# A transformer block kernel whose experts' second matrix becomes the moving operand, with tokens on the partitions

## The reference

```python
def _peer(h, w_q, sub_keys_1, sub_keys_2, expert_u, expert_v):
    ...                                   # choose 128 experts and gates per token
        u = expert_u[ix]
        v = expert_v[ix]
        a = jax.nn.gelu(jnp.einsum('td,thkd->thk', hx, u), approximate=False) * gx
        return jnp.einsum('thk,thkd->td', a, v)

    x = x + gate2 * _peer(h2, ...)        # end of the second block
return _rmsnorm(x, final_norm_g)          # mean of squares over 1024 features, then a gain

# linear attention: v is one quarter of the projection for each of 4 heads
proj = h @ w_in                           # gq, gk, gv, gr, glow, ..., iw, ...
```

## Time and profile before

| | us |
|---|---|
| median of three executions | 2174.11 |
| the profiled execution | 2175.14 |
| its span, first to last instruction | 2173.4 |
| TensorE busy | 2137.9 (98% of the span) |
| VectorE busy | 1609.3 (74%) |
| ScalarE busy | 967.6 (45%) |
| GpSimd busy | 401.8 (18%) |

### The profile page before, as it was taken

How to read it: one execution, slowest core, us unless ns; L and a number is a source line. 1 busy time by engine, 2 the same in 40 slices (tenths; PEclk the granted TensorE clock), 3 DMA queues, 4 the chain that set the end, 5 groups by cost and what they waited for, 6 DMA issues and landing times.

```text
span 2173.4 us, 30748 instructions
## 1 busy us (share of the span) xinstructions
PE 2137.9 (98%) x11787; PEld 1958.5 (90%) x11787; DVE 1609.3 (74%) x2958; ACT 967.6 (45%) x1689; POOL 401.8 (18%) x296
## 2 busy tenths in 40 slices
PE   8999989999999999999999999999999999999999
PEld 6877778887777788789999999999999999999998
DVE  4777556664976544799998897777667888888884
ACT  5444445444234423433364756766433333333333
POOL 2000110000000001000133333222223334443330
PEclk9999989999999999999999999999999999999999
DMA  7411135431231122124778888898999899999981
GB/s 257 148 50 40 49 128 192 170 136 61 104 106 41 51 85 97 64 95 146 256 279 282 307 290 284 302 314 292 333 355 385 345 375 365 370 374 376 375 334 57
DMA packets 137153, 471.07 MB, mean 217 GB/s; under 512 B 10080, under 2 KB 59488, under 8 KB 111280
## 3 DMA queue, kind: packets, MB, share of 16 engines
q1 hardware_dynamic: 45760, 283.96, 35.0%
q0 software_dynamic: 36864, 134.23, 16.4%
q10 hardware_dynamic: 54384, 50.92, 7.0%
HBM read 416.52 MB, written 52.43 MB: 216 GB/s over the span
## 4 chain that ended last, share of the span: by engine, by line
PE 84%; DVE 11%; ACTq 2%; ACT 1%; issue 1%; DMA 0%; SPq 0%; DVEq 0%
PE bank L156 83%; DVE whl L309 2%; ACTq L2235 2%; DVE L L1479 1%; DVE L L1477 1%; DVE row L2176 1%; DVE room L2120 1%; DVE room L2116 1%; PE bank L668 1%; DVE fg L2127 0%; PE bank L1568 0%; DMA XT<-in_xT 0%; DVE L L1460 0%; ACT whl L302 0%; DVE wk L1852 0%
## 5 line engine op out<-in xcount | busy, mean ns | idle before, releaser
L156 PE MATMUL bank<-xhl,whl 128*128 128x384 f32 (+1 forms) x5304 | 1092.3, 363 | 14.6 <-DVE whl L519 7.7
L156 PEld LDWEIGHTS bank<-xhl,whl 128*128 128x128 f32 x5304 | 948.9, 189 | 107.7 <-issue 11.0
L309 DVE TENSOR_TENSOR whl<-raw,whl 128x1024 fp32r<-128x1024 f32 (+2 forms) x389 | 469.1, 1215 | 254.1 <-ACT whl L302 208.5
L156 PE MATMUL bank<-ag,whl 128*128 128x384 f32 x3072 | 544.2, 340 | 1.3 <-ACT h_both L2231 1.3
L156 PEld LDWEIGHTS bank<-ag,whl 128*128 128x128 f32 x3072 | 542.1, 188 | 1.6 <-ACT h_both L2231 1.6
L302 ACT ACTIVATE whl<-raw 128x1024 fp32r<-128x1024 f32 (+2 forms) x389 | 398.0, 1034 | 217.7 <-PE bank L156 150.1
L2163 POOL DMA_INDIRECT row<-in_U_rows,row_at x128 | 182.1, 1423 | 607.6 <-DVE row L2176 432.3
L2163 POOL DMA_INDIRECT row<-in_V_rows,row_at x128 | 178.5, 1395 | 268.3 <-DVE y_tok L2192 236.3
L2192 DVE SCALAR_TENSOR_TENSOR y_tok<-row,row_a,y_tok 128x1024 f32<-128x1024 f32 x127 | 162.6, 1281 | 3.0 <-DMA row<-in_V_rows,row_at 0.3
L2176 DVE SCALAR_TENSOR_TENSOR row<-row,h_tok 128x1024 f32<-128x1024 f32 x128 | 155.7, 1218 | 0.4 <-DMA row<-in_U_rows,row_at 0.4
L156 PE MATMUL bank<-yhl,whl 128*128 128x512 f32 x540 | 132.3, 402 | 1.8 <-DVE whl L309 1.8
(11 more groups left out here) (257 smaller groups left out, 1932.2 us busy)
## 6 DMA issues: line engine op xcount, KB each, us to landing
raw<-in_U SPq DMA_DIRECT2D x64, 1024.0 KB
raw<-in_V SPq DMA_DIRECT2D x64, 1024.0 KB
hidden<-h_both ACTq DMA_DIRECT2D x32, 768.0 KB
gates<-g_stage ACTq DMA_DIRECT2D x12, 2048.0 KB, 15.0
g_ring<-gates SPq DMA_DIRECT2D x32, 768.0 KB
h_ring<-hidden SPq DMA_DIRECT2D x22, 768.0 KB, 7.8
raw<-in_w_ada SPq DMA_DIRECT2D x16, 1024.0 KB
raw<-in_w_gla SPq DMA_DIRECT2D x12, 1024.0 KB
```

The costliest lines, as they stand in the source:

```text
L156: return e.matmul(o, a, b, start=start, stop=stop, skip_group_check=True)
L309: e.tensor_tensor(lo[:, s], src[:, s], F(hi[:, s]), ALU.subtract).then_inc(dve_lo.of((i, half)))
```

## The change

**V stage.** V becomes the moving operand, 512 of the 1024 features at a time, and a 128 x 128 piece of `ag` (128 experts x 128 tokens) becomes the stationary one. The output has tokens on the partitions: three token blocks (`tb`) x two halves of the features, six PSUM banks. A group is 4 expert pieces x 3 token blocks x 3 products x 2 halves = 72 matmuls of 512 columns, 2304 in all; each stationary piece is loaded for two matmuls in a row, to two banks. The order in a group is n outside and token block inside, in the last group token block outside. `V` is laid out in memory for it; items keep their size. `act_gated` waits for piece n of the group before the last and no longer for its end.

**The end.** During groups 1 to 8 TensorE transposes x, a quarter of a bank at a time (32 transposes, L2380), and ScalarE copies it to `x_tok`; in groups 9 and 10 TensorE spreads the gate over all partitions (8 small matmuls) and ScalarE copies it to `gate_row`. The final gain comes by DMA as `norm_row`, 512 KB, on SyncE's queue in group 0. After the stream VectorE works on each token block in token layout: times gate (L2449), plus x (L2453), times root and gain (L2442); ScalarE squares and sums in one instruction (L2416) and takes the root. The rows' block (3) comes first, then 0 and 1 and at last block 2 by halves, whose second half ScalarE scales and writes from its own queue.

**The value item.** ScalarE's split of value item 0 is moved ahead of the copy of the index weights and of the Silu.

```diff
             copy(e, ik[0:64, :], gla_banks.of["small"][0:64, :]).then_inc(act_gla.of("ik"))
+            split_hi(e, q, IT["w_gla", 0] + 1)
             q.wait_ge(pe_gla["iw"])
...
-                split_hi(e, q, IT["w_gla", 3 * h] + 1)
+                if h > 0:
+                    split_hi(e, q, IT["w_gla", 3 * h] + 1)
...
-                    q.wait_ge(pe_v["y", g - 2, 7])
+                    q.wait_ge(pe_v["y", g - 2, n])
...
+                if g == 0:
+                    e.dma_start(norm_row, ins["norm_row"]).then_inc(in_norm.of("row"), 16)
...
-            y = [v_banks.fill(q, ("y", m)) for m in range(8)]
-            for g in range(NG):
-                for m in range(8):
-                    ...
-                    for n in range(4):
-                        o = half * 1024 + n * 256 + m % 2 * P
-                        x = mul3(e, y[m][:, 0:TD], (hi[:, o:o + P], lo[:, o:o + P]), (a_at(g, n, 0), a_at(g, n, 1)), ...)
-                    if g == NG - 1:
-                        e.transpose(y[m][:, TD:T], y_tok[:, m * P:(m + 1) * P], ident).then_inc(pe_v.of(("y", m)))
-                        if m >= 2:
-                            sums(m - 2)
-            for qt in range(NT):
-                for half in range(2):
-                    for c in range(4):
-                        m = e.transpose(b[:, c * P:(c + 1) * P], xt(4 * half + c)[:, qt * P:(qt + 1) * P], ident)
+            y = [[v_banks.fill(q, ("y", tb, half)) for half in range(2)] for tb in range(ND)]
+            def block(g, n, tb, halves):
+                i = IT["V", 2 * g + n // 2]
+                hi, lo = hi_lo(i)
+                q.wait_ge(act_hi[i, n % 2], dve_lo[i, n % 2], act_v["a", g, n], dve_v["a", g, n])
+                a, a_lo = (a_at(g, n, part)[:, tb * P:(tb + 1) * P] for part in range(2))
+                for x, w in ((a, hi), (a, lo), (a_lo, hi)):
+                    for half in halves:
+                        o = n % 2 * 1024 + half * 512
+                        m = mul(e, y[tb][half], x, w[:, o:o + 512], ...)
+                return m
+            for g in range(NG - 1):
+                for n in range(4):
+                    for tb in range(ND):
+                        m = block(g, n, tb, (0, 1))
+                    m.then_inc(pe_v.of(("y", g, n)))
+                    spent[IT["V", 2 * g + n // 2], n % 2] = pe_v, ("y", g, n)
+                if 1 <= g < 9:
+                    ...                       # four transposes of x
+                if 9 <= g < 11:
+                    ...                       # half of the gate, spread
+            g = NG - 1
+            for tb in range(ND):
+                for halves in ((0, 1),) if tb < ND - 1 else ((0,), (1,)):
+                    for n in range(4):
+                        m = block(g, n, tb, halves)
+                    m.then_inc(pe_v.of(("y", tb, halves)))
...
+            for qt in range(2):
+                q.wait_ge(pe_v["y", qt, (0, 1)])
+                gate_2(qt, (0, 1), [v_banks.of["y", qt, half] for half in range(2)]).then_inc(dve_v.of(("x4", qt)))
+                normed(3 if qt == 0 else 0)
+            q.wait_ge(pe_v["y", 2, (0,)])
+            gate_2(2, (0,), [v_banks.of["y", 2, 0]]).then_inc(dve_v.of(("x4", 2, 0)))
+            normed(1)
+            ...                               # both halves of block 2: L2484, L2449, L2453, root, scale
...
-    r["V"] = a["peer_v_2"][0].reshape(P, 32, 4, 2, 2, 256).transpose(1, 3, 0, 4, 2, 5).reshape(64, P, 2048)
+    r["V"] = a["peer_v_2"][0].reshape(P, 64, 2048).transpose(1, 0, 2)
+    r["norm_row"] = np.broadcast_to(a["final_norm_g_2"].reshape(1, 1024), (P, 1024))
```

More of the change, by code:

```diff
@@ L2383, in scalar_v @@
                         split_hi(e, q, i + 1, (m % 4 // 2,))
[L2384 to L2388, removed]
+                    if m == 3 and 2 <= g < 10:
+                        qt, half = (g - 2) // 2, (g - 2) % 2
+                        q.wait_ge(pe_v["x", qt, half])
+                        copy(e, x_tok[:, qt, 4 * half:4 * half + 4], by_chunk(v_banks.of["x", qt, half])
+                             ).then_inc(act_v.of(("x", qt, half)))
@@ L2389, in scalar_v @@
+                    if m == 3 and 10 <= g < 12:
+                        s = slice(512 * (g - 10), 512 * (g - 9))
+                        q.wait_ge(pe_v["gate row", g - 10], dve_row[P - 1])
+                        copy(e, gate_row[:, s], v_banks.of["gate row", g - 10]).then_inc(act_v.of(("gate row", g - 10)))
                     next(v, None)
             ready_root(e, q)
-            q.wait_ge(pe_v["sum", 7])
-            root(e, q, stat_a[:, 0:4], v_banks.of["sum"][:, 0:4], 1024).then_inc(act_v.of("root"))
@@ L2393, in scalar_v @@
[L2393 to L2397, removed]
-        def vector_v(e, q, rows):
+            for qt in (3, 0, 1):
+                q.wait_ge(dve_v["x4", qt])
+                e.activation(v_sq, last_at(qt), ACT.Square, accum_out=stat_a[:, qt:qt + 1]).then_inc(act_v.of(("square", qt)))
+                q.wait_ge(act_v["square", qt])
+                root(e, q, stat_a[:, 8 + qt:9 + qt], stat_a[:, qt:qt + 1], 1024).then_inc(act_v.of(("root", qt)))
@@ new lines, in scalar_v @@
+            for half in range(2):
+                s = slice(512 * half, 512 * half + 512)
+                q.wait_ge(dve_v["x4", 2, half])
+                e.activation(v_sq[:, s], last_at(2)[:, s], ACT.Square, accum_out=stat_a[:, 4 + half:5 + half]
+                             ).then_inc(act_v.of(("square", 2, half)))
+            q.wait_ge(act_v["square", 2, 1], dve_v["first half"])
+            e.activation(stat_a[:, 10:11], stat_a[:, 5:6], ACT.Sqrt, bias=stat_a[:, 4:5], scale=1.0 / 1024
+                         ).then_inc(act_v.of(("root", 2)))
@@ L2407, in vector_v @@
                         next(rows, None)
[L2408 to L2414, removed]
@@ L2415, in vector_v @@
-                    next(v, None)
[L2416 to L2422, removed]
+                    next(v, None)
@@ new lines, in vector_v @@
+            for _ in rows:
+                pass
+            q.wait_ge(dve_row[2 * P - 1], act_v["gate row", 1])
+            gate_2(3, (0, 1), [y_tok[:, 0:512], y_tok[:, 512:1024]]).then_inc(dve_v.of(("x4", 3)))
+            q.wait_ge(act_hi[len(PLAN) - 1, 1])
+            for qt in range(2):
+                q.wait_ge(pe_v["y", qt, (0, 1)])
+                gate_2(qt, (0, 1), [v_banks.of["y", qt, half] for half in range(2)]).then_inc(dve_v.of(("x4", qt)))
+                normed(3 if qt == 0 else 0)
```

93 lines of the change are left out of this document (64 added, 29 removed).

## The result

The changed kernel took 2159.93 us (median of four executions, 2159.22 to 2163.54) against 2174.11; the ratio is 0.9946, 95% interval [0.9929, 0.9964]. (The executions before are four: 2172.43 us belongs to them too.) I had forecast 2148.5, 25.6 us less; it became 14.2 less by the medians, and 11.7 by the ratio. In the profiled executions the time fell from 2175.14 to 2159.22, the span from 2173.4 to 2157.5: 15.9 us.

What follows compares the result with a forecast made beforehand. TensorE, busy 98% of the span, bounds the kernel by its matmul starts, standstills and end. -14.9 - 0.2 - 1.4 - 6.6 - 2.5 = -25.6 us, 2148.5 against 2174.11; own range 2142.5 to 2154, 8-in-10 range 2142 to 2161.

Steps and rivals of the forecast that it cites:

- I take 229.0: V stage: ns per 512-column matmul with whl moving over ag, chosen between bounds 226.9 and 234.3.
- the 227 to 231 named as the forecast's sign: V stage profile after: mean start distance in ns of a group's 72 matmuls, with no wait, expected if the forecast holds.
- the 240 that was to refute it: V stage profile after: a mean start distance above 240 ns was to refute the forecast.
- value item: Before the value projection: earlier split starts the 96 matmuls at 308.2 us, at full clock; -6.6 us, bounds -5.4 and 0.
- start of the stage: V stage start: TensorE takes six banks, so no wait for the U stage's last Gelu; -1.4 us.
- 2304 for 3072 matmuls: V stage stream: 527.6 us at 229.0 ns against 542.5 at 176.6; -14.9 us, with -19.7 and -2.7 at the bounds.
- added and removed inside: Inside the V stage: 40 small matmuls added (+4.9), transposes and square sums removed (-5.1); together -0.2 us.
- the end: After the last matmul: VectorE sets the end, 6.1 us behind, plus 3.1 for DMA, 9.2 against 11.7; -2.5 us.
- The line through the lengths: Unbroken streams of three lengths: 53 ns per 128 columns plus some 14 per matmul; 768 fewer matmuls save 10.7 us.
- What feeds the stream: V stage: VectorE at 88.4% and DMA share at 97% keep up with 16.5 us groups; costed at nothing.
- feeding: Rival, V stage: DMA or VectorE's order keeps a group at 16.95 us; +13.9 us, 2162.5; chance 0.08.
- columns are all that counts: Rival, V stage: a matmul costs what its columns cost, 235.5 ns; the 14.9 us are gone, 2163.4; chance 0.11.

Runs made afterwards that it cites:

- the repeated comparison: The changed kernel, unaltered, timed again beside the one with ag 32 bytes later on the same chip: 2157.83 us, ratio 0.9948 to the kernel before.

## Why the prediction was wrong

The direction and four of the five steps held. The 8-in-10 range of 2142 to 2161 holds 2159.93 only because it took in the rivals; the forecast's own, 2142.5 to 2154, doesn't. The step that failed is "I take 229.0, nearer to the low end, since `whl` as the moving operand shows none in either row": the stream measured 233.3, and this one term gave 9.9 us less than forecast, where 9.7 are missing in all. That is also outside the 227 to 231 named as the forecast's sign, and short of the 240 that was to refute it. By spans of the two profiles:

| step | forecast | measured | from |
|---|---|---|---|
| value item | -6.6 | -6.2 | next projection 326.4 to 319.99; end of the U stage 1612.5 to 1606.3 |
| start of the stage | -1.4 | -1.4 | gap before the stage 1.6 to 0.17 |
| 2304 for 3072 matmuls | -14.9 | -5.0 | 2304 x 233.3 against 3072 x 176.6 ns |
| added and removed inside | -0.2 | +0.1 | stage 547.8 to 542.9, less the stream |
| the end | -2.5 | -3.4 | 11.7 to 8.3 |
| sum | -25.6 | -15.9 | 2173.4 to 2157.5 |

**The stream's price.** Bounds and both their rows were right: 226.9 and 234.3, and it came to 233.3. What was wrong is the reason for the choice between them. I asked which role a tile has, and took the row with `whl` moving and 256 columns for the nearest. That row says nothing on 512: its stream takes 120.3 ns between starts with `yhl` 416 past a multiple of 512 from `whl`, 117.8 at 448 and 119.0 at 0, which doesn't follow the surcharge of 512 columns (7.5, 6.6 and none). The nearest row by the real cause was the other one, `yhl` over `whl` with 512 columns at 234.2: as many columns, and two tiles that lie 416 bytes past a multiple of 512 apart as `whl` and `ag` do, though in exchanged roles. Nothing in the trace named the distance, but two things in it were odd enough to ask: the same form of matmul had two prices by the names of its tiles, and the surcharge came in a regular pattern.

**The line through the lengths.** 53 ns for 128 columns and some 14 beside them was right (13.3 by the exact distances 120.0, 173.3 and 226.7). With the distance mended on both sides, 3072 x 173.3 = 532.4 us become 2304 x 226.7 = 522.3: -10.1, where I had 10.7 for the line. The isolated gap of the Trainium skill ("TensorE: Matmul & The Clock Gate", Back-to-back issue gap), N / 2.4 + 2.5 ns, would have made it 768 x 2.5 = 1.9, an estimate from that page; the runs disagree with it, by these 10.1.

**The time to compare with.** My 542.5 us for the old stream was true for the execution that I read and for one cluster of executions only. On the chip of the repeated comparison the changed kernel, at 2157.8, is 16.3 us under the upper cluster (median 2174.1) and 8.0 under the lower one (2165.9). The first four executions of the kernel before, 2172.4 to 2174.8, were all upper. Why an execution of the 384-column stream falls to one level or the other is open; the runs show only that at a distance of 0 modulo 512 it doesn't happen in twelve executions.

**What feeds the stream** I had at nothing, and it was nothing: no wait of TensorE in the whole stage at 233.3 ns. At 226.7, with the DMA engines at the same 0.94 of their time, five short waits of 2.3 us in total appear, and they are for ScalarE behind VectorE, not for a transfer. The rival 'feeding' is out for this change, and near: my 'costed at nothing' held at 228.9 and no longer at 226.7. In time the rivals 'feeding' (2162.5) and 'columns are all that counts' (2163.4) came nearer than the forecast, both by luck. Nothing waited; and the cost beside the columns was saved as forecast (768 x 13.3 = 10.2 us), but the new stream's surcharge of 6.6 ns against the old one's 3.3 took 5.1 of it back (2304 x 6.6 less 3072 x 3.3).

**The value item** moved as forecast, and the half-clock stretch behind the wait went with it: TensorE had been granted half the clock from 309.6 to 316.4 us, with no matmul started between 307.7 and 313.6, and is at full clock there after the change. The edit alone gave 5.5 to 5.9 us at the end by medians, though its ratio, over both clusters, doesn't exclude nothing.

**The end** was a little shorter than forecast: VectorE is 5.3 us behind TensorE, not 6.1 (a slower stream gives it 0.3 us more, and the sums of mine for handoffs were high), and the last DMA takes 3.0, not 3.1. That VectorE sets this end held.

The Trainium skill ("SBUF — State Buffer", Who interferes with whom) gives TensorE two independent read ports, one for the moving operand and one for weight loads, and names the port pair of VectorE and GpSimd as the only place of contention. The runs agree as far as others' traffic goes (233.3 with and without the rows' fetches). They are hard to square with two reads of TensorE that never touch each other: with only the distance between its two operands changed, 233.3 became 226.7. Where in the chip these 6.6 ns arise, no run shows.

## What to carry to other kernels

When one form of matmul has different prices for different tiles, work out where the tiles lie before choosing between the prices: here 96 unused bytes took the changed kernel from 2157.8 to 2142.5 us (ratios 0.9948 and 0.9891 to the kernel before, so 12 to 15 us), about as much as the whole rewrite had shown. Let the moving and the stationary operand lie a multiple of 256 bytes apart, above all behind a run of small tiles whose sizes are no multiples of it (256 rests on one execution, 0 on many). And before a stream's price is taken from one profile, run the old kernel often enough to see whether its times lie in one cluster.

## What the runs showed of the hardware that was not expected

- The distance between the moving and the stationary operand in a partition sets a surcharge on streams of fp32r with a weight load for each matmul. 512 columns, moving less stationary modulo 512 bytes: 226.7 ns at 0 and 256, 228.9 at 64, 233.3 at 96, 232.4 at 384 (all with `ag` stationary; 0 with `xhl` and `yhl` moving too), 234.2 at 416, 233.3 at 448 (both with `yhl` moving). It didn't change when both tiles moved by 32 bytes together, the only such move that was tried. Why it is so, and what lies between these points, is open.
- 384 columns with `ag` moving have two levels by execution, 173.3 and 176.6 ns, at 416; at 448 one profile has 176.7 and the times fall into two clusters as well; at 0 there is one cluster in twelve executions.
- With 256 columns (`whl` over `yhl`) 120.3, 117.8 and 119.0 ns at 96, 64 and 0: no such surcharge.
- Alternating two PSUM banks and loading one stationary piece twice in a row cost nothing: 226.7 with both, as in the `xhl` stream, which keeps to one bank and repeats one piece in three.
